# RMSNorm of the last stage: squares summed on ScalarE, the gain applied per partition after the transpose

## The reference

```python
mixed = concat([rms_norm(o_a, gout_a), rms_norm(o_b, gout_b)])   # two attention head groups
x = x + mixed @ w_out
hq = rms_norm(x, norm_mem_q)
mq = hq @ w_mq                                    # 4 heads of 128
s = einsum('bshd,bmhd->bhsm', mq, mkk) * 128 ** -0.5   # 256 memory tokens
mo = einsum('bhsm,bmhd->bshd', softmax(s), mvv)
x = x + mo @ w_mo
hf = rms_norm(x, norm_ffn)
x = x + (silu(hf @ w_gate) * (hf @ w_up)) @ w_down      # 2816 wide
return rms_norm(x, norm_final)
# rms_norm(x, g) = x * rsqrt(mean(x * x) + 1e-6) * g, over the 1024 features
```

## Time and profile before

| | us |
|---|---|
| median of 2 runs | 4176.1 (4160.1 to 4192.1) |
| the profiled execution, its own time | 4162.0 |
| its span, first to last instruction, slowest core | 4160.4 |
| spans of the eight cores | 4146.2 to 4160.4 |
| busy: PE / DVE / ACT | 3288.1 / 1879.6 / 1589.0 |
| chain that ended last, share: PE / DVE / ACT / issue | 63% / 16% / 10% / 8% |

### The profile page before, as it was taken

The page is one execution under the profiler, slowest core; times in us unless marked ns, Lnnn a source line. Parts: engine busy times, 40 slices in busy tenths (PEclk is TensorE's granted clock), DMA queues, the critical chain, the costliest instruction groups (busy, mean ns, idle before and its releaser), DMA issues.

```text
span 4160.4 us, 51848 instructions; the slowest of 8 cores (4146.2 to 4160.4 us)
## 1 busy us (share of the span) xinstructions
PE 3288.1 (79%) x15768; PEld 1405.2 (34%) x15768; DVE 1879.6 (45%) x3441; ACT 1589.0 (38%) x3348; POOL 21.4 (1%) x32
## 2 busy tenths in 40 slices
PE   1588888798831679999999953888887969696968
PEld 1244343444400233333333311333343424243433
DVE  5365563645625244545445452343434252524343
ACT  2254444544421347676776760211212121212121
POOL 0000000000000000000000000000000000000000
PEclk9986968979655999999999956899998989898989
DMA  4794000000010010000000005233333424242423
GB/s 137 114 111 45 7 1 1 1 1 1 1 18 0 1 13 1 5 1 1 1 1 1 1 8 134 84 144 117 112 117 112 126 103 144 92 159 82 157 98 110
DMA packets 88267, 245.51 MB, mean 59 GB/s; under 512 B 20848, under 2 KB 24432, under 8 KB 82800
## 3 DMA queue, kind: packets, MB, share of 16 engines
q1 hardware_dynamic: 70704, 211.90, 15.5%
q0 software_dynamic: 17296, 30.28, 6.3%
HBM read 255.65 MB, written 36.18 MB: 70 GB/s over the span
## 4 chain that ended last, share of the span: by engine, by line
PE 63%; DVE 16%; ACT 10%; issue 8%; DMA 2%; DVEq 1%; ACTq 0%; SPq 0%; POOLq 0%
PE ps L1138 8%; PE ps L1142 7%; PE ps L1158 6%; PE ps L819 6%; PE ps L797 5%; PE ps L804 3%; PE ps L523 3%; DVE arena L935 2%; PE ps L824 2%; PE ps L390 2%; PE ps L518 2%; PE ps L413 2%; PE ps L550 2%; PE ps L1073 2%; PE ps L683 2%
## 5 line engine op out<-in xcount | busy, mean ns | idle before, releaser
L808 ACT ACTIVATE arena<-ps 128x512 bf16<-128x512 f32 x1024 | 553.8, 594 | 191.8 <-PE ps L804 191.2
L830 DVE TENSOR_TENSOR arena<-arena 128x512 f32<-128x512 f32 x480 | 332.5, 693 | 356.0 <-ACT arena L808 352.7
L819 PE MATMUL ps<-arena 128*128 128x512 bf16 x1024 | 393.4, 384 | 0.6
L528 ACT ACTIVATE arena<-ps 128x192 bf16<-128x192 f32 (+2 forms) x944 | 256.0, 322 | 346.8 <-PE ps L523 339.7
L1145 ACT ACTIVATE arena<-ps 128x512 f32<-128x512 f32 x176 | 105.1, 597 | 694.8 <-PE ps L1138 694.7
L1147 DVE TENSOR_TENSOR arena<-ps,arena 128x512 bf16<-128x512 f32 x176 | 121.8, 692 | 532.1 <-PE ps L1142 507.6
L1138 PE MATMUL ps<-arena 128*128 128x512 bf16 x1408 | 346.0, 390 | 10.0 <-ACT arena L973 10.0
L1142 PE MATMUL ps<-arena 128*128 128x512 bf16 x1408 | 336.5, 382 | 0.0
L1158 PE MATMUL ps<-arena 128*128 128x512 bf16 x1408 | 309.9, 379 | 8.1 <-DVE arena L1161 8.1
L797 PE MATMUL ps<-arena 128*128 128x512 bf16 x1024 | 304.6, 379 | 0.0
L523 PE MATMUL ps<-arena 128*128 128x192 bf16 (+2 forms) x944 | 184.1, 285 | 92.0 <-DVE arena L495 61.0
(11 more groups left out here) (157 smaller groups left out, 4080.6 us busy)
## 6 DMA issues: line engine op xcount, KB each, us to landing
arena<-wg_bf SPq DMA_DIRECT2D x176, 256.0 KB, 3.6
arena<-wu_bf SPq DMA_DIRECT2D x176, 256.0 KB, 3.5
arena<-x SPq DMA_DIRECT2D x64, 512.0 KB, 4.7
arena<-wd_bf SPq DMA_DIRECT2D x16, 2048.0 KB, 9.6
arena<-wo_bf SPq DMA_DIRECT2D x8, 2048.0 KB, 9.5
out<-arena SPq DMA_DIRECT2D x32, 512.0 KB, 2.7
arena<-wd_bf SPq DMA_DIRECT2D x8, 1536.0 KB, 6.9
wg_bf<-w_gate POOLq DMA_DIRECT2D x1, 5632.0 KB, 60.4
```

Of the source, the lines that this page charges most:

```text
L808: P.op('act', (lambda t: lambda e: e.activation(out=PT5[pis[t]], in_=ps[banks[t]][:, :], func=AF.Exp, scale=SC_B))(t), reads=[psb[banks[t] ...
L819: P.op('pe', (lambda kt, pi: lambda e: e.matmul(out=ps[nb][:, :], lhsT=vtok[:, kt, :], rhs=PT5[pi], start=(kt == 0), stop=(kt == 31)))(kt, ...
L830: P.op('dve', (lambda pi: lambda e: e.tensor_tensor(out=ad, in0=ad, in1=PT5[pi], op=ALU.add))(pi), reads=[B_PT5[pi], bad], writes=[bad])
```

## The change

Three edits, all in the last stage, and a new input.

- Statistics: act_stats takes the place of rms_stats4 in norm_pre and in the final norm. It sums the squares by an ACT Square of 128 x 1024 with accum_out; the sqrt (ACT) and the reciprocal (DVE) follow as before. The norm of the memory tokens (norm_T4) keeps rms_stats4.
- norm_pre multiplies by rstd alone (tensor_scalar); the gain is left out there.
- norm_post rotates over four PSUM banks, 4 to 7, and evacuates each of the eight 128 x 128 blocks by an ACT activation Copy of its own. Its scale is the gain as a column, since features lie on the partitions after the transpose.
- gcols2 (128 x 16, float32) holds the two gains as columns; it is loaded on SP at the start, behind gcols and into the same Buf. The loads of gmq and gff stay.

```diff
+    gc2 = AR.view(8000, [128, 16], F32)
...
     P.dma('sp', gc, gcols, writes=[B_gc])
+    P.dma('sp', gc2, gcols2, writes=[B_gc])
...
+    def act_stats(ap_, bufs_):
+        k = tl['st'] % 6
+        tl['st'] += 1
+        col = small[:, 8 + 4 * k:8 + 4 * k + 1]
+        bb = B_small[8 + k]
+        P.op('act', lambda e: e.activation(out=junk2, in_=ap_, func=AF.Square, accum_out=col), reads=bufs_, writes=[B_junk2, bb])
+        P.op('act', lambda e: e.activation(out=col, in_=col, func=AF.Sqrt, bias=EPS, scale=1.0 / D), reads=[bb], writes=[bb])
+        P.op('dve', lambda e: e.reciprocal(out=col, in_=col), reads=[bb], writes=[bb])
+        return col, bb
+
     def norm_pre(ap_, bufs_, gtile):
-        cols, bb = rms_stats4([(ap_, bufs_)])
+        col, bb = act_stats(ap_, bufs_)
         k = tl['x4'] % 4
         tl['x4'] += 1
-        P.op('dve', lambda e: e.scalar_tensor_tensor(out=xn2[k], in0=ap_, scalar=cols[0], in1=gtile, op0=ALU.mult, op1=ALU.mult),
-             reads=list(bufs_) + [bb, B_g3], writes=[B_xn2[k]])
+        P.op('dve', lambda e: e.tensor_scalar(out=xn2[k], in0=ap_, scalar1=col, scalar2=None, op0=ALU.mult),
+             reads=list(bufs_) + [bb], writes=[B_xn2[k]])
         return k
 
-    def norm_post(k, dstT, i, dst_buf):
-        pb = 4 + tl['pT'] % 2
+    def norm_post(k, dstT, i, dst_buf, g0):
+        pb = 4 + tl['pT'] % 4
         tl['pT'] += 1
         for c in range(8):
             P.op('pe', (lambda c: lambda e: e.transpose(out=psT[pb][:, c, :], in_=xn2[k][:, c * 128:(c + 1) * 128], identity=ident))(c),
                  reads=[B_xn2[k], B_const], writes=[psb[pb]])
-        P.op('act', lambda e: e.copy(out=dstT[:, :, i * 128:(i + 1) * 128], in_=psT[pb]), reads=[psb[pb]], writes=[dst_buf])
+        for c in range(8):
+            P.op('act', (lambda c: lambda e: e.activation(out=dstT[:, c, i * 128:(i + 1) * 128], in_=psT[pb][:, c, :], func=AF.Copy,
+                                                         scale=gc2[:, g0 + c:g0 + c + 1]))(c),
+                 reads=[psb[pb], B_gc], writes=[dst_buf])
...
-            norm_post(nslots[tt], hg, tt, B_hg[tt])
+            norm_post(nslots[tt], hg, tt, B_hg[tt], 0)
...
-            norm_post(nslots[tt], hg, tt, B_hg[tt])
+            norm_post(nslots[tt], hg, tt, B_hg[tt], 8)
...
-                    cols, bb = rms_stats4([(x1[:, tt, :], [B_x1[tt]])])
+                    col, bb = act_stats(x1[:, tt, :], [B_x1[tt]])
+                    cols = [col]
```

More of the change, by code:

```diff
@@ L223, in build @@
     gcols = din("gcols", [128, 16])
+    gcols2 = din("gcols2", [128, 16])
     g_mix = din("g_mix", [1, D])
@@ L1209, in prep_inputs @@
     gcols[:, 14] = np.tile(np.concatenate([-np.ones(32, np.float32), np.ones(32, np.float32)]), 2)
+    gcols2 = np.zeros((128, 16), np.float32)
+    gcols2[:, 0:8] = f(inputs['norm_mem_q'])[0].reshape(8, 128).T
+    gcols2[:, 8:16] = f(inputs['norm_ffn'])[0].reshape(8, 128).T
     shared = {
-        'cst': make_consts(), 'gcols': gcols,
+        'cst': make_consts(), 'gcols': gcols, 'gcols2': gcols2,
         'g_mix': f(inputs['norm_mix']).reshape(1, D), 'g_memq': f(inputs['norm_mem_q']).reshape(1, D),
```

## The result

| | before | after |
|---|---|---|
| profiled execution, its own time | 4162.0 us | 4272.3 us |
| span of the slowest core | 4160.4 | 4270.8 |
| spans of the eight cores | 4146.2 to 4160.4 | 4255.8 to 4270.8 |
| mean granted clock of PE | 0.88 | 0.87 |

The ratio of times is 1.0266, 95% interval 1.0218 to 1.0314. Forecast: 4294, +132; the profiled times differ by 110.

A forecast was written before the change was run, and what follows sets the result against it. It took the chain of waits as the bound, with DVE on the path in 12 tiles a group and ACT's evacuation in 2 batches. 4162.0 + 157.0 - 25.5 - 7 + 6 + 1 = 4293.5, say 4294 us; range 4235 to 4345.

The forecast's parts named there:

- Term 1: Evacuation in norm_post: eight ACT instructions in place of one copy cost 9.81 us more in each of 16 batches, +157.0 us.
- Term 2: Scale in norm_pre: tensor_scalar takes 753 ns, 0.53 us less than the STT, in 48 tiles, -25.5 us.
- Term 3: Squares moved to ACT: DVE loses 1.3 us of work but waits as long; -0.07 us a tile, 96 tiles, -7 us.
- Term 4: PE's clock at L1073 and L1138: ten microseconds more idle time makes the slow start lose 3.0 us at both, +6 us.
- Term 5: Start of the kernel: the gcols2 load waits for gcols, one more small transfer ends near 16 us, +1 us.
- Rival A: Evacuations: ACT's waits on its own instructions cost nothing, so 4210 us (+1.2%), not slower by 2%; chance 0.10.
- C: Evacuations: the pointer's time alone is hidden behind the wait, so 4252 us, still over 2%; chance 0.06.
- B: Statistics on ACT: Square or Copy missing from sqrt's table set, two table loads a tile, +225 us, 4519; chance 0.04.

The follow-up runs named there:

- experiment 1: Changed kernel with a separate bookkeeping buffer for each 128x128 block of hg, so evacuations don't wait on each other; 4186.6 us, ratio to the kernel before 1.0058.
- experiment 2: Changed kernel with an immediate scale of 1.0 in the eight evacuations, gain left out there, waits kept; 4223.2 us.
- experiment 3: Kernel before with only the new eight-part evacuation; squares stay on DVE, scale by scalar_tensor_tensor with a tile of ones; 4316.5 us.
- experiment 6: Changed kernel with the eight evacuations of a tile undone to one ACT copy, four banks kept, gain left out; 4105.5 us, ratio to the kernel before 0.984.
- experiment 5: Kernel before with norm_pre's scale by tensor_scalar, gain left out, squares on DVE, one copy a tile; spans of 4111.0 to 4120.2 us on cores 4 to 7.
- experiment 4: Kernel before with only the squares moved to ACT, in norm_pre and the final norm; 4147.4 us.
- experiment 7: Kernel before with squares on ACT, each tile's reciprocal and scale after the next tile's adds, tile tt-2 transposed and copied in the loop; second time 4007.5 us, ratio 0.9654.
- experiment 8: Kernel before with the new order of experiment 7 but squares left on DVE; 4088.6 to 4101.8 us on cores 4 to 7.
- experiment 9: Loop of experiment 7 in the kernel of experiment 1: gain at the evacuation, eight evacuations a tile without waits; 4036.7 to 4047.9 us on cores 4 to 7.

## Why the prediction was right, and where it was not

- **Term 1, the evacuation (+157).** Right, by the mechanism and the size. 366 ns measured, 367 taken; 32 in 14.00 us, 13.98 taken. Experiments 1 and 2 show the wait and the pointer at their prices (86 and 49 us), experiment 3 the whole at +154. The four banks brought what was said: nothing while ACT is the bound, and with one copy a tile 0.3 to 0.5 us a batch (experiment 6, against experiment 5 with two banks and against the kernel before).
- **Term 2, the scale (-25.5).** Right: 753 ns, as worked out; 4.15 us a tile in experiment 5.
- **Term 3, the squares (-7).** The step held: DVE waits 1.64 us (1.86 with the table loads shared out) where it worked 1.3 and waited 0.40. The read of the accumulator exists and takes 187 ns. Sqrt follows the second add by 1.33 us instead of 1.43, not 1.36; the term is -10. Periods 4.59 and 4.06 us, 4.6 and 4.1 predicted.
- **Term 4, PE's clock (+6). This step was wrong**, in sign. I took a longer idle time to mean a longer slow start. The stretches that hang on the clock are 1.6 us a group shorter on core 5 (cross-attention 1.2, behind it 0.2, Silus 0.2) and 2.3 on core 3, so -13 to -18. That is a difference of some 19 to 24 us, as much as the forecast was too high by (22). The time came within 22 us although the sign of this term was wrong because the term is small beside term 1. The windows of that stretch on the slowest core of each, 3185 to 3211 us before and 3236 to 3261 after (busy time of PE, PEld, DVE, ACT, POOL; granted clock; DMA):

```profile
3185.00:3211.00 26.00, 18.16 (x62) 6.54 (x63) 2.77 (x4) 12.92 (x22) 0.00 (x0) 0.82 0.00 0
```

```profile
3236.00:3261.00 25.00, 16.59 (x62) 6.38 (x65) 3.25 (x5) 12.55 (x22) 0.00 (x0) 0.90 0.00 1
```

In finer windows, first before and then after, one sees what the term had not thought of, a second fall of the clock from full to half speed, in the midst of the cross-attention:

```profile
3193.00:3196.00 3.00, 2.56 (x12) 0.98 (x10) 0.00 (x0) 1.36 (x3) 0.00 (x0) 1.00 0.00 0
3196.00:3199.00 3.00, 1.16 (x3) 0.43 (x4) 0.00 (x0) 2.17 (x3) 0.00 (x0) 0.77 0.00 0
3199.00:3202.00 3.00, 2.50 (x7) 0.69 (x5) 0.35 (x1) 2.28 (x5) 0.00 (x0) 0.66 0.00 0
```

```profile
3246.00:3249.00 3.00, 0.71 (x5) 0.37 (x5) 0.00 (x0) 2.63 (x4) 0.00 (x0) 1.00 0.00 0
3249.00:3252.00 3.00, 1.92 (x9) 0.59 (x8) 0.69 (x1) 2.69 (x5) 0.00 (x0) 1.00 0.00 0
```

- **Term 5, the start (+1).** The loads of gcols and gcols2 together kept SP until 13.7 us, and the last work before the barrier, on DVE, ended at 15.7 instead of 15.4. It cost at most 0.3 us.
- **Rival A** (waits for free) fell in experiment 1, **C** (pointer hidden) in experiment 2. **B** (table loads) fell in the trace: 16 loads at the sqrt and one at the memory norm, as before, and none at L967 or L987. The first statistics of a boundary show what a load costs on the path:

```profile
3189.43 0.19 ACT L967 ACTIVATION_READ_ACCUMULATOR arena<-arena 128x1 f32 x1
3189.70 1.28 ACT L968 ACT_TABLE_LOAD   x1
3190.99 0.20 ACT L968 ACTIVATE arena<-arena 128x1 f32<-128x1 f32 x1
```

It is 1.28 us, and Sqrt starts 0.01 behind it. ScalarE: Activation LUTs in the Trainium skill (What ACT_TABLE_LOAD costs) gives about 2.66 us, drain included; the trace doesn't show them here.

**The clock in the cross-attention.** The means of this stretch hide two kinds of it. The twelve traces have 640 of them (first cast of mq to last Exp, one for each group and core that is read). 483 have no second fall and 157 have one, which begins 12.2 to 13.1 us behind the start of mq's matmuls. Those without take 18.0 to 19.0 us, those with it 19.6 to 20.7, and none lies between. What goes ahead differs too: counted from the same start, the clock had risen from half to full speed after at most 5.55 us in those without a second fall and after 5.36 to 6.31 in those with it. How many of each kind a kernel has:

| | tile period ahead, us | with a second fall |
|---|---|---|
| before | 4.69 | 39 of 64 |
| evacuation alone (experiment 3) | 4.69 | 48 of 64 |
| squares alone (experiment 4) | 4.59 | 19 of 64 |
| scale alone (experiment 5) | 4.15 | 9 of 32 |
| changed kernel, and one copy (experiment 6) | 4.06 | 0 of 64 each |
| no waits, immediate (experiments 1 and 2) | 4.06 | 8 and 2 of 64 |
| new order (experiment 7, the second time) | no one period | 17 of 64 |
| new order (experiments 8 and 9) | no one period | 6 and 4 of 32 |

So the slow start itself was not longer with 12 us of idle time ahead but shorter, 4.3 us on average against 5.4, and the second fall, which 39 of 64 stretches had, was gone. The 32 matmuls of mq, forecast near 9.9 us, took 9.0 on average on core 5 (9.6 before). In the old order the second falls get fewer as the tiles ahead go faster, and the idle time in between does not decide it. What makes a start long or short, and why experiment 7 has second falls again, stays open. Cores of one execution differ as well (18.7 to 19.3 us on average in experiment 4), so the steps between the means of core 5 alone say little.

## What to carry over

An engine's queue is in order: work taken from an engine that then waits for the result shortens nothing until its next instructions are put ahead of that wait. Here the same move of the squares was worth 12 to 15 us in the old order and 96 in the new. A copy split into eight pays each time for its fixed part, its pointer operand, and any wait that the bookkeeping puts between writes of one buffer, even to disjoint parts; one buffer for each part took 86 of 110 us away again.

## What was not expected of the hardware

- PE's slow start was not longer with 12 us of idle time right ahead of it than with transposes and 1.25 us of idle time ahead: L1089's mean matmul is 452 ns against 472 for L1073 on core 5 (256 each).
- Without a wait, ACT instructions of 128 columns with a pointer scale start every 0.25 us while each lasts 479 ns on average from start to end, and longer the later it comes in its batch; the duration of a single one says nothing on its rate.
- The cross-attention behind mq is of two kinds in time, 18.0 to 19.0 or 19.6 to 20.7 us, by whether PE's clock falls a second time in it.
